# Sample recurrence and mixer norm placed inside the chunks of the prompt recurrence

## The reference

```python
o, S = gated_delta_chunked(q, k, v, g, beta, S0, chunk)
o = rms_norm(o, gdn_norm) * jax.nn.silu(g_z.reshape(B, T, GDN_HEADS, GDN_DV).astype(f32))
...
y, h = ssd_chunked(xs, dt, -jnp.exp(ssm_A_log.astype(f32)), bh, ch, h0, chunk)
y = (y + ssm_D[:, None] * xs).reshape(B, T, SSM_INNER) * jax.nn.silu(s_z.astype(f32))
y = rms_norm(y.reshape(B, T, SSM_GROUPS, SSM_INNER // SSM_GROUPS),
             ssm_norm.reshape(SSM_GROUPS, -1)).reshape(B, T, SSM_INNER)
mix = jnp.concatenate([o.reshape(B, T, GDN_VW), y], axis=-1).astype(x.dtype) @ w_out
return x + mix, (S, gdn_conv, h, ssm_conv)
```

```python
S_t = a_t S_{t-1} + beta_t k_t (v_t - k_t^T a_t S_{t-1})^T,  o_t = S_t^T q_t
h_t = exp(dt_t A) h_{t-1} + dt_t x_t B_t^T,  y_t = h_t C_t
```

## Time and profile before

| | us |
|---|---|
| median of 3 runs | 1588.0 (1587.28 to 1588.25) |
| the profiled execution | 1588.74 |
| its span | 1587.1 |
| busy in the span: PE, DVE, ACT, POOL | 1519.4, 755.2, 593.4, 160.3 |

### The profile page before, as it was taken

One profiled execution on the slowest core, in us unless ns is written; L12 is line 12 of the kernel. 1 busy time (PEld: TensorE's weight loads), 2 busy tenths in 40 slices (PEclk: granted clock), 3 DMA queues, 4 the chain that ended last, 5 costly groups with the idle time before them and its releaser, 6 DMA issues.

```text
span 1587.1 us, 29335 instructions
## 1 busy us (share of the span) xinstructions
PE 1519.4 (96%) x11922; PEld 1420.7 (90%) x11922; DVE 755.2 (48%) x1268; ACT 593.4 (37%) x906; POOL 160.3 (10%) x193
## 2 busy tenths in 40 slices
PE   7999988887999999999999999999899999999999
PEld 7999978885779999999999967677799999999998
DVE  7677466664773444443232326455434444443222
ACT  5344432223424434432222364356434443442211
POOL 1000022220620000000010000353020000000000
PEclk9899999999999999999999999899899999999999
DMA  6122200003243332333332420365322233322332
GB/s 217 56 91 79 81 1 1 1 1 124 66 144 106 87 93 93 93 93 96 93 90 83 122 75 33 94 178 156 129 74 82 91 93 93 93 93 86 88 95 77
DMA packets 46592, 140.27 MB, mean 88 GB/s; under 512 B 6768, under 2 KB 16080, under 8 KB 45616
## 3 DMA queue, kind: packets, MB, share of 16 engines
q1 hardware_dynamic: 40128, 114.38, 23.7%
q0 software_dynamic: 6096, 20.60, 4.2%
q10 hardware_dynamic: 288, 4.19, 0.7%
HBM read 130.34 MB, written 7.76 MB: 87 GB/s over the span
## 4 chain that ended last, share of the span: by engine, by line
PE 86%; DVE 6%; ACT 3%; issue 3%; DVEq 0%; DMA 0%; POOL 0%; ACTq 0%; POOLq 0%
PE PS L509 84%; DVE arena L1662 1%; PE PS L994 1%; DVE arena L1730 0%; ACT wsplit L1149 0%; DVE arena L1657 0%; DVE arena L1652 0%; DVE arena L1768 0%; DVE wsplit L1573 0%; DVE arena L1749 0%; DMA gains<-in_gains 0%; ACT arena L1472 0%; ACT rinv L1136 0%; DVE arena L1801 0%; ACT arena L1281 0%
## 5 line engine op out<-in xcount | busy, mean ns | idle before, releaser
L509 PE MATMUL PS<-xnh,wsplit 128*128 128x260 f32 x3904 | 638.1, 285 | 14.2 <-DVE wsplit L1573 11.3
L509 PEld LDWEIGHTS PS<-xnh,wsplit 128*128 128x128 f32 x3904 | 541.5, 190 | 16.2 <-DVE wsplit L1573 11.8
L509 PE MATMUL PS<-xnl,wsplit 128*128 128x260 f32 x1952 | 395.0, 284 | 0.0
L1149 ACT ACTIVATE wsplit<-wring 128x1024 fp32r<-128x1024 f32 x176 | 182.9, 1041 | 450.0 <-PE PS L509 443.1
L1573 DVE TENSOR_TENSOR wsplit<-wring,wsplit 128x1024 fp32r<-128x1024 f32 x176 | 211.0, 1200 | 215.7 <-ACT wsplit L1149 215.7
L509 PEld LDWEIGHTS PS<-xnl,wsplit 128*128 128x128 f32 x1952 | 302.5, 190 | 0.0
L509 PE MATMUL PS<-hidh,wsplit 128*128 128x260 f32 x1408 | 226.6, 283 | 0.0
L509 PE MATMUL PS<-arena 128*128 128x128 f32 (+4 forms) x1328 | 199.6, 316 | 14.5 <-DVE arena L1730 6.6
L509 PEld LDWEIGHTS PS<-arena 128*128 128x128 f32 (+2 forms) x1328 | 166.6, 199 | 45.1 <-issue 25.0
L509 PEld LDWEIGHTS PS<-hidh,wsplit 128*128 128x128 f32 x1408 | 192.9, 188 | 0.0
L509 PE MATMUL PS<-hidl,wsplit 128*128 128x260 f32 x704 | 141.3, 282 | 0.0
(11 more groups left out here) (364 smaller groups left out, 1658.3 us busy)
## 6 DMA issues: line engine op xcount, KB each, us to landing
wring<-in_w_gu SPq DMA_DIRECT2D x88, 512.0 KB, 3.5
wring<-in_w_dn SPq DMA_DIRECT2D x32, 512.0 KB, 3.5
wring<-in_w_proj SPq DMA_DIRECT2D x28, 512.0 KB, 3.6
wring<-in_w_dn SPq DMA_DIRECT2D x16, 384.0 KB, 3.1
wring<-in_w_outa SPq DMA_DIRECT2D x8, 512.0 KB, 3.6
wring<-in_w_inc SPq DMA_DIRECT2D x8, 512.0 KB, 3.5
wring<-in_w_uq SPq DMA_DIRECT2D x8, 512.0 KB, 4.7
wring<-in_w_outc SPq DMA_DIRECT2D x8, 512.0 KB, 4.2
```

Source lines behind the costliest of these rows:

```text
L509: return pe.matmul(out, lhsT, rhs, start=start, stop=stop)
L1149: act.activation(dst[:, 0:w], wring[u][:, 0:w], ACT.Copy).then_inc(s('w_hi'), 1)
```

## The change

The sample step is moved into the chunks, and the mixer norm is done for one chunk while the next one runs. In words, by engine:

- SP loads the sample states in four halves of 1 MB into the weight ring, as it comes free after the input projection, and the weights of `outa` after them (`state_half`). POOL's own loads of `s0` and `h0` for the update stay where they are; POOL's decays wait for them and for `MIXED - 1` parts of the split of `mix`.
- DVE prepares the sample's scalars before the last projection tile (`sample_tables`); PE spreads them ahead of chunk 0.
- After level 3 of chunk c PE multiplies one half of a state (`state_products`), ACT copies the rows, after level 4 PE turns them (`turn_rows`), and DVE combines them (`sample_step`): chunks 0 and 1 do GDN, 2 and 3 SSD. DVE's `hssd` update moves ahead of that, from after level 5 to after level 4.
- ACT squares chunk c - 1 at the head of chunk c, PE takes the means in level 5 (`mix_means`), ACT the roots before its copy of `w` (`mix_root`), DVE scales ahead of its state update (`chunk_scaled`). Chunk c - 2 is split at the head (`chunk_high`) and in level 1 (`mix_low`). The rest of chunk 3 and the samples follow at the end.
- `outa` takes the contraction's tiles in the order 4 to 7, 0 to 3; the first half waits for all but the last part of the split.

The diff, cut to its core:

```diff
 @sync
+            def state_half(k):
+                dst, seqs = halves[k % 2], slice(4 * (k % 2), 4 * (k % 2) + 4)
+                if k < 2:
+                    sp_.dma_start(dst.rearrange(...), A['s_gdn'][:, :, seqs]).then_inc(s(f'half_loaded{k % 2}'), 16)
+                else:
+                    sp_.dma_start(dst.rearrange(...), A['s_ssm'][:, seqs]).then_inc(s(f'half_loaded{k % 2}'), 16)
...
+                if before == 'proj':
+                    for k in range(2):
+                        for u in (2 * k, 2 * k + 1):
+                            sp_.wait_ge(*slot_freed('proj', TURNS['proj'] - 1, u))
+                        state_half(k)
+                    for k in (2, 3):
+                        sp_.wait_ge(s('sv_mm'), 2 * (k - 2) + 1)
+                        state_half(k)
...
+                    elif before == 'proj':
+                        sp_.wait_ge(s('sv_mm'), 5 if u < 2 else 7)
 @gpsimd
-            pool.wait_ge(s('sv_mm'), 1)
-            pool.wait_ge(s('y0_mm'), 1)
-            pool.wait_ge(s('mix_split'), KD - 1)
+            pool.wait_ge(s('st_loaded'), 16)
+            pool.wait_ge(s('h0_loaded'), 16)
+            pool.wait_ge(s('mix_split'), MIXED - 1)
 @tensor
                         if mixed is not None:
-                            pe.wait_ge(s('mix_split'), mixed + k + 1)
+                            k = (n + 4) % KD
+                            pe.wait_ge(s('mix_split'), MIXED - 1 if n < 4 else MIXED)
...
+            pe.wait_ge(s('sprep_ready'), 1)
+            mm(PS[:, 7, 0:192], const('ones')[0:8, :], valx[0:8].rearrange("p a b -> p (a b)"))
+            for m in range(4):
+                for e in range(2):
+                    at_ = 192 + (m * 2 + e) * NS
+                    mm(PS[:, 7, at_:at_ + NS], tabs[0:8, e, m * 128:(m + 1) * 128], ident[0:8, 0:8])
+            mm(PS[:, 7, 256:288], const('ones'), qkp.rearrange("p a b -> p (a b)"))
+            mm(PS[:, 7, 288:304], const('ones'), bcp.rearrange("p a b -> p (a b)")).then_inc(s('spread_mm'), 1)
+
+            def state_products(k):
+                pe.wait_ge(s(f'half_loaded{k % 2}'), 16 * (k // 2 + 1))
+                pe.wait_ge(s('rhs2_ready'), 1)
+                pe.wait_ge(s('yt_taken'), k + 1)
+                vectors = rhs2 if k < 2 else cpad
+                for j in range(4):
+                    ...
+                    ins = mm(PS[32 * j:32 * j + 32, 0, :], vectors[:, 4 * (k % 2) + j, :], states)
+                ins.then_inc(s('sv_mm'), 1)
+
+            def turn_rows(k):
+                pe.wait_ge(s('spread_ready'), k + 2)
+                for h in range(4):
+                    ins = pe.transpose(PS[:, 0, h * 128:(h + 1) * 128], rows[:, h * 128:(h + 1) * 128], ident)
+                ins.then_inc(s('sv_mm'), 1)
+
+            def mix_means(e):
+                pe.wait_ge(s('l2sq_ready'), 8 + e + 1)
+                pe.wait_ge(s('h_ready'), e + 2)
+                mm(PS[:, 1, :], const('ones_128'), sq8[:, 0:4, :])
+                pe.wait_ge(s('vnt_ready'), e + 2)
+                for o in range(2):
+                    ins = mm(PS[:, 0, 0:256], const('ones_256'), sq8[:, 4 + o::2, :], o == 0, o == 1)
+                ins.then_inc(s('l2_mm'), 1)
...
+                    if l == 5 and c:
+                        mix_means(c - 1)
...
+                    if l == 3:
+                        state_products(c)
+                    if l == 4:
+                        turn_rows(c)
...
+                else:
+                    pe.wait_ge(s('l2sq_ready'), 8 + 4)
+                    for o in range(2):
+                        mm(PS[:, 4, 0:272], const('ones_256'), sqa[:, o::2, :], o == 0, o == 1)
+                    mm(PS[:, 4, 272:304], const('ones_128'), sqs).then_inc(s('l2_mm'), 1)
 @scalar
+            def chunk_high(e):
+                act.wait_ge(s('mix_ready'), e + 1)
+                act.activation(mixh[:, :, es], mix[:, :, es], ACT.Copy).then_inc(s('xn_hi'), 1)
+
+            def mix_root(n, *parts):
+                act.wait_ge(s('l2_mm'), 8 + n + 1)
+                for out, mean in parts:
+                    ins = act.activation(out, mean, ACT.Ln, bias=small[:, C_EPS:C_EPS + 1])
+                ins.then_inc(s('ln_ready'), 1)
+                act.wait_ge(s('ln_ready'), R_MIX + n + 1)
+                whole = root8 if n < 3 else roota if n == 3 else rootb
+                act.activation(whole, whole, ACT.Exp, scale=-0.5).then_inc(s('rinv_ready'), 1)
...
+                if c:
+                    ...
+                    act.activation(sq8, mix[:, :, (c - 1) * 128:c * 128], ACT.Square).then_inc(s('l2sq_ready'), 1)
+                if c >= 2:
+                    chunk_high(c - 2)
...
+                    if l == 3:
+                        act.wait_ge(s('sv_mm'), 2 * c + 1)
+                        act.activation(rows[:, :], PS[:, 0, :], ACT.Copy).then_inc(s('spread_ready'), 1)
+                if c:
+                    mix_root(c - 1, (root8[:, 0:256], PS[:, 0, 0:256]), (root8[:, 256:768], PS[:, 1, :]))
                 act.wait_ge(s('w_mm'), c + 1)
                 act.activation(wt, PS[:, 3, :], ACT.Copy, scale=-1.0).then_inc(s('w_ready'), 1)
+                if c == NCH - 1:
+                    ...
+                    act.activation(sqa, mix[:, 4:8, 384:TOK], ACT.Square)
+                    act.activation(sqs, mix[:, 0:4, T:TOK], ACT.Square).then_inc(s('l2sq_ready'), 1)
+                    act.wait_ge(s('qe_ready'), NCH)
+                    high('outa', 0, 0)
 @vector
+                def between():
+                    if c == 0:
+                        sample_vectors()
+                    elif c >= 2:
+                        mix_low(c - 2, (slice(0, KD), slice((c - 2) * 128, (c - 1) * 128)))
+                def states():
+                    dve.wait_ge(s('hup_mm'), c + 1)
+                    st.sync()
+                    st(tt(hssd, hssd, PS[:, 1, :], ALU.add), s('h_ready'))
+                    sample_step(c)
-                fill = {0: ssd_scores, 2: ssd_out, 3: queries}
+                fill = {0: ssd_scores, 1: between, 2: ssd_out, 3: queries, 4: states}
...
+                if c:
+                    chunk_scaled(c - 1)
+                if c == NCH - 1:
+                    low('outa', 0, 0)
+                    dve.wait_ge(s('rinv_ready'), R_MIX + 4)
+                    ssd_scaled(slice(384, TOK), roota[:, 0:272].rearrange("p (g n) -> p g n", g=2))
+                    gdn_scaled(sc, by(roota[:, 272:304], GH))
+                    mix_low(2, (slice(0, KD), slice(256, 384)))
                 dve.wait_ge(s('kv_mm'), c + 1)
...
+            mix_low(3, (slice(4, 8), slice(384, TOK)), (slice(0, 4), sc))
+            dve.wait_ge(s('rinv_ready'), R_MIX + 5)
             dve.wait_ge(s('ot_taken'), NCH)
+            gdn_scaled(slice(384, T), by(rootb, GH))
+            mix_low(4, (slice(0, 4), slice(384, T)))
+            low('outa', 0, 1)
```

More of the change, by code:

```diff
@@ L519, in piece @@
                 def piece(p, u, chunks, k0, last, done, norm=None, mixed=None):
-                    for k in range(chunks):
+                    for n in range(chunks):
+                        k = n
                         if norm is not None:
@@ L681, in _ @@
                             pe.wait_ge(s('x_ready'), n - 1)
[L682 to L683 removed]
+                        elif half:
+                            pe.wait_ge(*((s('s_ready'), c) if c else (s('spread_ready'), 1)))
                         for h in (2 * half, 2 * half + 1):
@@ L1318, in _ @@
-            act.wait_ge(s('y0_mm'), 1)
-            act.activation(hrow, PS[:, 6:8, :], ACT.Copy).then_inc(s('spread_ready'), 1)
+            act.wait_ge(s('mix_ready'), 4)
+            act.activation(mixh[:, 4:8, 384:TOK], mix[:, 4:8, 384:TOK], ACT.Copy)
+            act.activation(mixh[:, 0:4, T:TOK], mix[:, 0:4, T:TOK], ACT.Copy).then_inc(s('xn_hi'), 1)
+            mix_root(4, (rootb, PS[:, 5, :]))
+            act.wait_ge(s('mix_ready'), 5)
+            act.activation(mixh[:, 0:4, 384:T], mix[:, 0:4, 384:T], ACT.Copy).then_inc(s('xn_hi'), 1)
@@ L1331, in mix_root @@
-            def mix_root(e):
-                act.wait_ge(s('l2_mm'), 8 + (e + 1 if e < 4 else 4 + 2 * (e - 3)))
-                if e >= 2:
-                    act.wait_ge(s('mix_ready'), e - 1)
-                rsqrt(R_MIX + e, two(rinv[:, (R_MIX + e) % 2, :]), bank2(4 + 2 * (e % 2)))
-            for j in range(8):
-                if j >= 2:
-                    act.wait_ge(s('l2_mm'), 8 + j - 1)
-                act.activation(sq[:, j % 2, :], mix[:, j, :], ACT.Square).then_inc(s('l2sq_ready'), 1)
-                if 1 <= j <= 4:
-                    mix_root(j - 1)
-                elif j == 6:
-                    mix_root(4)
-                if j == 2:
-                    for u in range(2):
-                        high('outa', 0, u)
-                if 3 <= j <= 6:
-                    mix_high(j - 3, (s('mix_ready'), j - 2))
@@ L1349, in _ @@
-            mix_root(5)
-            for k in range(4, KD):
```

(43 more changed lines are left out.)

259 lines of the change are left out of this document (99 added, 160 removed).

## The result

The changed kernel takes 1577.07 us, the median of four runs (1573.77 to 1578.70), beside 1588.12 of the kernel before on the same chip (1587.28 to 1588.36): a ratio of 0.9921, with a 95% interval of 0.9898 to 0.9944. It is 11 us faster where 20 were forecast, 0.07 us above the upper end of the forecast's range (1577). The profiled execution took 1573.77, the lowest of the four (span 1572.1).

A forecast was written before the change was run, and what follows sets the result against it. The prediction saw a chain of short dependent steps before `outa`, PE mostly waiting, as removable, and PE or the PE-ACT-DVE loop pacing the recurrence: 1588.74 - 32.7 + 9.75 + 2.15, taken as 1568 us; range 1561 to 1577.

The forecast's parts named there:

- The recurrence: Four prompt chunks: chunks 1 to 3 grow 2.75 us each, chunk 0 by 0.95 + 0.55; total +9.75, bounds 6 to 12.
- The 0.42: Level 4 of a chunk: its second half starts some 0.42 us late, after DVE's subtraction, so new products net 0.55.
- The rule on draining: `state_products` in each chunk: two more tiling-mode changes at 0.17 us would add 1.4, giving 1569.4; left out.
- the 0.96 forecast: Level 3 of each chunk: the eight instructions of `state_products` take 0.96 us, half of a measured 1.92.
- The new tail: Last `w` product to `outa`: start at w + 10.8 instead of w + 43.5, 32.7 us less, SSD half first.
- What is late next: Output projection: `h0` lands 4.15 us later against PE, 2.0 of slack, so PE stalls 2.15; bounds 0 to 6.
- the sentence on the stores: Output projection: DVE's first residual waits for stores some 3.5 us later than the tile; the next tile's 7.87 covers that.
- POOL's lateness reaching PE behind the fifth tile: Output projection: POOL's late decays delay `update(3)`, whose sum PE needs after the fifth tile; PE stalls 2.15 us.
- A: Rival, chance 0.13: half clock from waiting in level 5 and the tail, four stretches of 1.7 us, 6.8 more: 1574.8.
- B: Rival, chance 0.08: `h0` shares DMA with output weights, takes 18 us instead of 9, all reaching PE: 1577.
- C: Rival, chance 0.03: clock stays at 1.2 GHz through the recurrence, making it slower than before: 1608.
- D: Rival, chance 0.02: the removed stretch before `outa` is not on the end's path: 1588.

The follow-up runs named there:

- the delayed kernel: The changed kernel with 2.4 us of extra, overwritten PE products at 885 us, behind the projection and ahead of the attention: 1575.06 us.
- stores moved: The changed kernel with the two stores of the prompt's states issued on POOL ahead of the load of `h0`: 1579.07 us.
- a fill: Extra PE products with unread results in the idle before the attention's first transposes; six products: 1571.79 us in the changed kernel, 1591.29 in the kernel before.

## Why the prediction was right, and where it was not

*Direction and mechanism*: right. The chain from the last state update to `outa` was on the end's path, and taking it out gave what it held.

*The recurrence*, forecast +9.75, measured +8.40. The growth of a chunk was sized well: at full clock 39.53 became 42.51, so 2.98 where 2.75 was forecast; at a clock of 0.96, 41.18 became 44.06, 2.88. The difference is chunk 0 and the clock. Up to chunk 0's copy of `w` the kernels differ by 0.45 (240.70, 241.15) where 1.50 was forecast; and over chunks 1 to 3, 8.25 were forecast and 7.96 came, as chunk 2 of the changed profile had no half-clock stretch, where each of these chunks before had one. The 0.42 that PE is said to wait in level 4 is not in the earlier trace rows, where 64 instructions stand in one row without an idle; without it the forecast would be 3.17 a chunk. The rule on draining, which would have made it 1.4 more, was rightly left out. In chunk 2 the product's eight instructions stand between its neighbours without an idle:

```profile
318.37 1.07 PE L540 MATMUL PS<-ring_words,cpad 128*32 128x512 f32 x8
319.37 3.24 PE L540 MATMUL PS<-arena 128*128 128x128 f32 x24
```

The next group starts 1.00 us after the product does, against the 0.96 forecast. The Trainium skill, TensorEngine Tiling (Array Packing), Key Properties, says that a change of mode drains TensorE; the trace leaves a drain at most 0.04 a chunk beyond the 0.96, which was half of a group with its own entry and exit, so what a drain costs in all, these rows do not show. The 0.17 that the prediction calls an idle of PE is one of its weight loads (PEld in the earlier trace rows).

*The new tail*: `outa` at `w` + 10.64, forecast 10.8, and no wait between the SSD and the GDN half. Right to 0.2 us.

*What is late next*, forecast +2.15, measured +3.26 in the profile. The step that failed is the sentence on the stores: "some 3.5 later than the tile; the next tile", 7.87 long, "covers that". DVE runs in order: its first residual did not only free the first tile's bank, the first sample's update was queued behind it, and PE needs that update's sums right behind the second tile. From the residual to the end of the first sum DVE takes 3.9 us (392.23 to 395.28 + 0.84), so the next tile covers about 4.0 and not 7.87. The store came 4.2 behind the tile in the changed kernel's profile, and PE waited; it came 3.5 behind it in the delayed kernel's, and PE did not. The prediction named the wait and did not name what is queued behind it. The step next to it, POOL's lateness reaching PE behind the fifth tile, was right, with a size too small, and hidden: the loss at the second tile gave POOL the time that it lacked. Without that loss it came out at 3.59 us (stores moved) and 3.73 (store in time) where 2.15 was forecast. The forecast had no term for the clock behind a stall, which cost more than the wait (some 3.2 of the 4.0).

*The rivals*. A had the right kind of loss, half clock, in the wrong place: the recurrence had no more of it, the projection and the attention had. B's condition did not come: `h0` landed 8.8 us after its issue, where B had 18; what cost was the store behind it. C and D are out.

*The missing 6.2 us*. The second step that failed is a term that is not in the sum: the stages behind the projection stand in it at nothing, and no rival has them. Their code is unchanged, and that was enough up to the attention's transposes (533.58 and 533.58). From there its time is one of two values: in the nine profiles without a fill 579.2 (three) or 585.2 to 585.4 (six), by when PE's idle of 1.63 us comes. The changed kernel came there at the worse moment in both of its profiles, the kernel before, in its profile, at the better. The delays show it: 1.2 us added to the kernel before bring 585.2 and 5.9 us in the time. The changed kernel with 2.4 added has 579.15, but there PE came 8.05 later, so this profile shows that the change does not force the early fall, and not what 2.4 us do. What makes a moment a bad one, no run shows. The range went up to 1577 for other reasons, and that the median lies no further from it is luck.

*Open*. The medians differ by 11.0 and the profiled executions by 15.0, since the changed kernel's profiled execution was its fastest. Where its other executions lose the 3 us more is not shown by a profile of one of them; the projection of 74.8 us in the delayed kernel, 3.8 longer by the wait behind the fifth tile and the clock after it, is a candidate.

## What to carry to other kernels

When a stage is moved earlier, list for each engine what is queued behind every wait that stays where it was, a store's landing too; when the first late thing is mended, look for the second in the same trace before trusting the gain. Split a difference of times into stages at places that both profiles have, and if a stage with unchanged code differs, look at the granted clock first: a kernel can win or lose more there than by the edit under test, as the one with the old contraction order did. Where PE idled just ahead of sparse work and the clock fell early, a few products of filling made the time lower here, the fewer that fit the idle at least as much; in the kernel where the clock did not fall early, filling cost its delay and more.

## What was not expected of the hardware

An addition of 1.2 us of work made a kernel 5.9 us slower, through the granted clock some hundred us further on, and one of 2.4 us made another no slower (1.3 us lower, with overlapping spreads). PE counts as busy without a gap from the transposes on (3.00 of 3.00 us in each window above), and yet in the late fall the clock fell near the end of the 32 products of 16 columns, with no idle in the 6.0 us before it. POOL's decays of 128x512 took 1.05 us each in some stretches and up to 2.04 in others, with DVE busy beside them; which of DVE's operations slow them was not tried.
